# A decoder layer on one core: expert weights in 2 MB instead of 4 MB transfers from the eighth expert on

## The reference

```python
def expert_block(args):
    xb, e = args
    hgl = xb @ w1[e] + b1[e]                       # w1[e]: 1024 x 2048, 8 MB
    glu = jnp.minimum(hgl[:, :D_EXPERT], SWIGLU_LIMIT)
    lin = jnp.clip(hgl[:, D_EXPERT:], -SWIGLU_LIMIT, SWIGLU_LIMIT)
    act = glu * jax.nn.sigmoid(SWIGLU_ALPHA * glu) * (lin + 1.0)
    return act @ w2[e] + b2[e]                     # w2[e]: 1024 x 1024, 4 MB
```

## Time and profile before

| | before |
|---|---|
| median of 3 executions | 1338.08 us (1337.27 to 1339.41) |
| the profiled execution, its own time | 1339.8 us |
| span of the profiled execution (first to last instruction) | 1338.0 us |
| around the span | 1.8 us |
| PE busy | 1294.3 us (97%) |
| share of the span on the chain that ended last: PE, DMA | 72%, 23% |
| expert weights by 4 MB transfers | 46 of `w_expert_in`, 23 of `w_expert_out` |

### The profile page before, as it was taken

The page is one execution under the profiler, slowest core; times in us unless marked ns, Lnnn a source line. Parts: engine busy times, 40 slices in busy tenths (PEclk is TensorE's granted clock), DMA queues, the critical chain, the costliest instruction groups (busy, mean ns, idle before and its releaser), DMA issues.

```text
span 1338.0 us, 17324 instructions
## 1 busy us (share of the span) xinstructions
PE 1294.3 (97%) x7364; PEld 718.2 (54%) x7364; DVE 423.8 (32%) x803; ACT 326.1 (24%) x533; POOL 38.3 (3%) x64
## 2 busy tenths in 40 slices
PE   8999999999999999999999999999999999999997
PEld 7999999999998333333333333333333333333332
DVE  6775777586453212111121121111121111112111
ACT  5865456554443111000010001000001000001102
POOL 2002210001000000000000000000000000000000
PEclk9999999999999999999999999999999999999999
DMA  7556544569868899999999999999999999999995
GB/s 230 158 189 216 164 139 145 159 189 373 287 238 345 359 430 428 418 434 431 432 430 430 432 431 432 433 432 432 431 432 432 432 431 432 432 432 430 427 425 244
DMA packets 89074, 474.79 MB, mean 355 GB/s; under 512 B 7414, under 2 KB 69014, under 8 KB 70584
## 3 DMA queue, kind: packets, MB, share of 16 engines
q1 hardware_dynamic: 88320, 470.71, 86.8%
q10 hardware_dynamic: 696, 3.24, 0.7%
HBM read 472.86 MB, written 1.07 MB: 354 GB/s over the span
## 4 chain that ended last, share of the span: by engine, by line
PE 72%; DMA 23%; DVE 2%; ACT 2%; issue 0%; ACTq 0%; DVEq 0%
DMA arena<-in_w_expert_in 22%; PE ps L1044 21%; PE ps L1098 13%; PE ps L656 7%; PE ps L657 6%; PE ps L658 6%; PE ps L1004 3%; PE ps L984 3%; DVE w_lo L1606 1%; PE ps L1012 1%; PE ps L996 1%; PE ps L1074 1%; PE ps L647 1%; PE ps L648 1%; PE ps L649 1%; PE ps L1068 1%
## 5 line engine op out<-in xcount | busy, mean ns | idle before, releaser
L1044 PE MATMUL ps<-arena 128*64 128x512 f32 x2048 | 462.0, 607 | 24.9 <-DMA arena<-in_w_expert_in 24.4
L1044 PEld LDWEIGHTS ps<-arena 128*64 128x64 f32 x2048 | 148.5, 140 | 330.9 <-issue 291.0
L1948 DVE TENSOR_SCALAR arena<-ps 128x512 f32<-128x512 f32 x32 | 22.1, 692 | 664.5 <-PE ps L1044 664.5
L1098 PE MATMUL ps<-arena 128*64 128x512 f32 x1024 | 227.0, 595 | 0.0
L656 PE MATMUL ps<-A_hi,w_hi 128*128 128x256 f32 x576 | 165.3, 287 | 1.9 <-DVE w_lo L1606 1.9
L1606 DVE TENSOR_TENSOR w_lo<-w_raw,w_hi 128x1024 fp32r<-128x1024 f32 x120 | 146.3, 1260 | 64.6 <-ACT w_hi L1237 64.3
L657 PE MATMUL ps<-A_lo,w_hi 128*128 128x256 f32 x576 | 162.9, 283 | 0.0
L658 PE MATMUL ps<-A_hi,w_lo 128*128 128x256 f32 x576 | 162.9, 283 | 0.0
L1098 PEld LDWEIGHTS ps<-arena 128*64 128x64 f32 x1024 | 70.7, 137 | 135.6 <-issue 135.5
L1483 ACT ACTIVATE arena<-arena 128x512 f32<-128x512 f32 x32 | 20.1, 630 | 478.5 <-DVE arena L1948 478.5
L1237 ACT ACTIVATE w_hi<-w_raw 128x1024 fp32r<-128x1024 f32 x120 | 120.4, 1049 | 29.5 <-DMA w_raw<-in_w_fox_branch 6.6
(11 more groups left out here) (307 smaller groups left out, 1257.4 us busy)
## 6 DMA issues: line engine op xcount, KB each, us to landing
arena<-in_w_expert_in SPq DMA_DIRECT2D x46, 4096.0 KB, 37.2
arena<-in_w_expert_out SPq DMA_DIRECT2D x23, 4096.0 KB, 39.4
arena<-in_w_expert_in SPq DMA_DIRECT2D x26, 2048.0 KB, 17.2
w_raw<-in_w_in SPq DMA_DIRECT2D x32, 1024.0 KB, 5.3
arena<-in_w_expert_in SPq DMA_DIRECT2D x20, 1024.0 KB, 8.3
arena<-in_w_expert_out SPq DMA_DIRECT2D x10, 2048.0 KB, 14.9
arena<-in_w_expert_out SPq DMA_DIRECT2D x16, 1024.0 KB, 20.1
w_raw<-in_w_cross_kv SPq DMA_DIRECT2D x8, 1024.0 KB, 7.6
```

The source lines that it names most:

```text
L1044: last = mm(ps[64 * half:64 * (half + 1), b, :], xg_cols[:, 2 * h + c, s, :], columns[:, :, half, :], start=False, stop=(s + h + c == 3), ...
L1098: last = mm(ps[64 * half:64 * (half + 1), bank, :], cols[:, c, h, :], w[:, at:at + 512], start=(h + c == 0), stop=(h + c == 4))
L1948: V_.tensor_scalar(glu, ps[:, 0, :], LIMIT, None, ALU.min).then_inc(glu_ready, 1)
```

## The change

`BY_HALF` becomes 96, so `by_half(n)` is true for every chunk. The number of experts ahead of the hardware loop, which was derived from it, is set to the same 7. Nothing else is edited; `whole` stays in use only for items beyond the 32nd, which these inputs don't have.

```diff
-BY_HALF = 21
-LAST_TWO = CHUNKS * (NE - 2)
+BY_HALF = CHUNKS * NE
...
         def by_half(n):
-            return n < BY_HALF or n >= LAST_TWO
+            return n < BY_HALF
...
-            looped = BY_HALF // CHUNKS
+            looped = 7
```

## The result

| | before | changed |
|---|---|---|
| median of 6 executions each | 1338.47 us (1336.23 to 1341.34) | 1343.86 us (1342.33 to 1346.41) |
| ratio, 95% interval | | 1.0041 (1.0026 to 1.0055) |
| the profiled execution: own time, span | 1339.8, 1338.0 us | 1344.18, 1342.4 us |

The changed kernel is slower by 0.41%, 5.5 us by the ratio, with an interval of 3.5 to 7.4 us. The two profiled executions differ by 4.4 us.

A forecast was written before the change was run, and what follows sets the result against it. The prediction took the weight stream as the bound once PE had caught up; 5.0 us of longer stream less 1.7 us of PE slack gave +3.3 us, so 1341.4 us, range 1339.2 to 1344.2.

The forecast's parts named there:

- The bound: Expert stage: PE sets the pace at first, then, once caught up, the weight stream at 29.14 us an expert.
- The price of a pair: Weight stream: two halves take 0.067 to 0.075 us more than a whole chunk; over 69 pairs, 5.0 us later landings.
- The first rival: Weight stream doesn't get longer, the transfer cost being hidden in the queue; PE gains 1.7 us: 1336.4 us, chance 0.08.
- the one by the windows: Weight stream: the trace windows' rates are right and halves slow it by 9.5 us; +7.8, 1345.9 us, chance 0.05.
- Transfers that each start from rest: Weight stream: each of 69 added transfers pays 4.8 us beyond its own transfer; 331 us more, 1667 us, chance 0.01.
- The fit of 2.0 us plus bytes over 436 GB/s: Skill page's cost of a DMA; if each new transfer in the stream paid it, 69 x 2.0 = 138 us slower.
- The queues at nothing: SP's load queue: 69 more issues at 0.33 us each, hidden by the queue ahead of them, cost nothing.
- The waits: PE's load waits: two or three an expert, none above 1.5 us, one new before output 31's first quarter.
- The rival by the clock: Last two experts: new PE waits lower the clock, so the end comes another 1.7 us later: 1343.1 us, chance 0.08.
- The end of the last output matmuls: Expert 31's last output matmuls, behind its quarters' landings, end at 1331.5 us instead of 1328.13.
- The slack of 1.7 us: First quarter of output 31: PE uses it 1.7 us after landing, so this comes off the stream's 5.0 us.
- the last term of the sum: Behind the last output matmuls: the rest to the end is a chain of small steps that doesn't change, so nothing.

The follow-up runs named there:

- e6_last_four: The kernel before with halves for the last four experts instead of the last two; ratio to the kernel before 1.0006 (0.9989 to 1.0024).

## Why the prediction was right

Forecast were 1341.4 us, 3.3 more than before; measured were 1343.86, 5.4 more by the medians and 4.4 in the profiled pair. The mechanism held, and the size came out too small.

- **The bound.** The stream sets the pace from about 840 us on, and everything behind it moves with its last landing. This held in every run above.
- **The price of a pair**, read from the halves on either side, was 0.067 to 0.075 us; over the whole stretch it was 9.789 - 9.713 = 0.076. For the stream I took 5.0 us and it was 5.3. The first rival (no longer stream) is out, and so is the one by the windows: the late stretch that had given 425 GB/s before moves at 428 in the changed kernel, with the same transfers. The landings before say 428 too (2 MB in 4.894 us), so 425 was the reading of a short window, and it was right to use it as a bound only. Transfers that each start from rest are out by the 4.89 us from landing to landing. The fit of 2.0 us plus bytes over 436 GB/s that the prediction cites stands on the Trainium skill's page "DMA: Bandwidth & Descriptors" in the section Anatomy of one DMA — SWDGE (gpsimd) path, and was taken on DMAs that GpSimd issues; here SP issues them.
- **The queues at nothing.** SP's issues lengthened up to 1.8 us in places, and the landings stayed 4.89 us apart. The stage paced by PE kept its pace, with the start of the stream at the same time as before.
- **The waits.** Forecast: more numerous, none over 1.5 us, a new one in front of the first quarter of output 31, less of the low clock. All came: 31 of at most 1.2 us, 0.6 us in front of that quarter, clock 1.00. The rival by the clock is out for this execution: expert 30 had two new waits, of 1.1 and 1.2 us, and the clock stayed at 1.00. But the forecast had PE ready 2 us ahead of the quarter's landing, less four transposes, and it was 0.5 ahead (1321.77 against 1322.25).
- **The end of the last output matmuls** was forecast at 1331.5 and came at 1331.94. The slack of 1.7 us was indeed used up, less the 0.14 us that PE takes to start behind a landing. That it exists was rightly read, why it does was not: it was one fall of the clock at 1255.8, as the run without the branch showed. So the 1.7 us that the sum takes off belong to the execution that was profiled, and that they fitted the pair was partly luck. In an execution without that fall the kernel before should end sooner, at its own branch: 3.5 us from the last landing to the scatter, as in e6_last_four, instead of 4.4. The difference would then be about 5.3 us, an estimate. How often that happens is not known from single profiles. It would raise the difference of the medians, which is 5.4 us against 4.4 in the pair; that it is the reason is not shown, and the interval (3.5 to 7.4) holds both.
- **The step that was mis-sized** is the last term of the sum: "The rest to the end is a chain of small steps which doesn't change." It was put at nothing, and it contains a branch of 3.4 to 3.8 us that starts at the last landing. It was covered while PE ran 3.7 us behind that landing, and no longer when it ran 2.3 behind: 0.8 us. From the scatter to the end it took 0.2 us less than before. So +3.8 for the matmuls, +0.8, -0.2 make the 4.4 us of the profiled pair, where I had forecast 3.3.

## What to carry to other kernels

Where a stream of loads is the bound, as here, its price is in bytes and in packets: read the distance between landings for each row length that the kernel already uses, and multiply. Finer transfers pay only where a consumer stands still for the missing part at the end; in the middle they move idle time about. And before something is counted as slack, see what hides under it: here a branch that started at the same landing came out as soon as PE was closer behind it. Slack read from one execution can also be the trace of something that another execution doesn't have, here one fall of the clock.

## What was not expected of the hardware

- Each packet of a saturated stream costs about 9.5 ns of its DMA engine beyond its bytes (an estimate), the same from 32 to 16 KB as from 16 to 8 KB: 9.713, 9.789 and 9.940 us for 4 MB.
- Transfers to 64 of the 128 partitions ran at half of the rate (206 to 214 GB/s).
- A taken branch over a long block of TensorE's code held its queue for 3.36 to 3.83 us in ten executions and ended 1.4 us behind a 16 KB fetch of instructions; one that was not taken, 0.07 us.
- Behind a wait of 2.3 us the clock was at its lower level for a part of the next 32 matmuls in one execution (8.78 us) and not in another (7.09 us), at the same place of the program. Within one execution, too, a wait of 2.33 us left it alone (7.09 us, at 993.53).
